# Matmuls that nobody reads, in the norms of a two-block transformer kernel

## The chip, the cores and the metric

One core of one Trainium2 chip runs the whole kernel. The metric is the device time of one execution in microseconds; the kernel before takes 1953.42 us (median of 3 runs, 1952.22 to 1953.73).

## The reference, cut to what matters

256 tokens of width 1024 go through two layers of a first block and two layers of a second block, all in float32. Ahead of nearly every large product stands an RMS norm over the 1024 channels of a token:

```python
def rms_norm(x, gain):
    xf = x.astype(jnp.float32)
    y = xf * lax.rsqrt(jnp.mean(xf * xf, axis=-1, keepdims=True) + EPS)
    return (y * gain.astype(jnp.float32)).astype(x.dtype)
...
# first block, twice: norm1, mixer (delta rule and short convolution), w_out, norm2, feed-forward
h = rms_norm(x, norm1_g);  proj = h @ w_in;  ...;  x = x + mixed @ w_out
h2 = rms_norm(x, norm2_g)
x = x + (jax.nn.silu(h2 @ ffn_w_gate) * (h2 @ ffn_w_up)) @ ffn_w_down
...
# second block, twice: three sub-layers (feed-forward, mixer, feed-forward), each of this form
def pre(x_in, i):
    return rms_norm_2(x_in, norm_pre[l, i]) * (1.0 + mod[:, i, 1]) + mod[:, i, 0]
def post_add(x_in, y, i, res_w):
    return x_in + res_w * mod[:, i, 2] * rms_norm_2(y, norm_post[l, i])
```

So there are ten norms ahead of products: four in the first block (two in each layer), six in the second (three in each layer).

## The kernel before, in words

**Order of the work.** The program is a list of steps (block, layer, kind, number), written out by hand. Each engine runs through the same list and issues its own part of each step; semaphores tie the parts together. Nothing is scheduled by a tool.

**Products.** Every weight matrix comes from memory in units of 128 x 1024. ScalarE rounds a unit to the short float32 form (`w_hi`, L983), VectorE subtracts to get the rest (`w_lo`, L1334), and TensorE multiplies high by high, high by low and low by high. In the feed-forwards (`gu` steps) one pair of matmuls does this for one block of 128 channels: 512 columns against `w_hi` (L515) and 256 columns against `w_lo` (L516); a first `gu` step has 16 such pairs. In the mixers a block takes three matmuls of 256 columns (L609 to L611 in their first step, L505 to L507 later). The sums with the tokens on the partitions (`out`, `mout`, `down`) are matmuls of 512 columns; the last of them are L545 to L547.

**A norm ahead of products** (kinds `norm` and `pre`) takes its input from such sums. VectorE adds them to `x` (L1468), or, from the second block's first feed-forward on, a `post` step does this and the norm behind it in one chain of VectorE and ScalarE. ScalarE sums the squares, VectorE scales four quarters of `x` into `xs` (L1357, a part of the tensor `mx`; in the fused chain the last quarter comes from ScalarE, L1039). TensorE turns each quarter with four transposes of 128 x 128 (L689; `q` counts the quarters). When quarter 2 is turned, ScalarE and VectorE read the turned tiles out of PSUM into `hf`, apply the gain (L1099, L1102, L1409, L1411) and split them into `h_hi` and `h_lo` (L1108, L1044, L1342). The next step's first product waits for the first `h_lo`.

**Names.** `quad` is four PSUM banks that the products of the steps use in turn; `banks[0]` and `banks[1]` count how often each half of it has been read out. `works` (also `work[0]` to `work[3]`) is the other four banks. `n["turn"]` counts the norms ahead of products (0 to 9), `FUSED` is 5: the norms of turn 5 and later follow a `post` step directly. `g_hi` is a buffer of rounded hidden values, `ident_r` the rounded identity.

Of the kernel before, what the change touches and what calls it, by code (L numbers as in the profile page):

```python
# [205 lines left out]
def build(nc, w, x_in, const_in, p1_in, p2_in, bt_in, out):  # L206
    with ExitStack() as ctx:
        def sb(name, shape, dt=F32):
            return ctx.enter_context(nc.sbuf_tensor(name, shape, dt))

        def ps(name, shape):
            return ctx.enter_context(nc.psum_tensor(name, shape, F32))
# [11 lines left out]
        g_hi = sb("g_hi", [P, 4, T], F32R)  # L224
# [17 lines left out]
        ident_r = sb("ident_r", [P, P], F32R)  # L242
# [3 lines left out]
        quad = ps("quad", [P, 4, 512])  # L246
        stream = [quad[:, 2 * i, :].rearrange("p (a t) -> p a t", a=2) for i in range(2)]
        works = ps("works", [P, 4, 512])
        work = [works[:, i, :] for i in range(4)]
# [34 lines left out]
        def turned_tile(into, kt):  # L284

            at = kt % 4 // 2 * T
            return into[2 * (kt // 4) + kt % 2][:, at:at + T]
# [113 lines left out]
        banks = [s_bank0, s_bank1]  # L401
# [8 lines left out]
        FUSED = AT[2, 0, "pre", 0]["turn"] + 1  # L410

        def scaled_before(turn):
            return 4 * turn - max(turn - FUSED, 0)

        chunks, loads = [], []
        for B, L, kind, i, n in NUMBERED:
# [5 lines left out]
            else:  # L422
                for v in range(n["split"], n["split"] + units_of(B, kind, i)):
                    if v % 2 == 0:
                        loads.append(("raw", len(chunks)))
                        chunks.append(("split", v + 2))
        chunk_of_unit = [c for c, (kind, _) in enumerate(chunks) if kind == "split" for _ in range(2)]
        chunk_of_mod = {n - 1: c for c, (kind, n) in enumerate(chunks) if kind == "mod"}
        mod_of_side = {k: m for m, k in SIDE_OF.items()}
# [65 lines left out]
        def _(pe):  # L495
            mm, tr = nc.tensor.matmul, nc.tensor.transpose
# [38 lines left out]
            def product_rows_end(unit, kts, r_hi, r_lo, sums):  # L535

                pe.wait_ge(s_lo_ready, unit + 2)
                for q in range(2 * TT):
                    for e, kt in enumerate(kts):
# [10 lines left out]
                        elif e:  # L550
                            last.then_inc(s_bank_done, 1)

            def attend(L, k, h0):

                kp, ke = k // 2, k % 2
                pe.wait_ge(s_pt_sb, AH * L + k + 1)
                if ke == 0:
                    pe.wait_ge(s_hf_done, h0 + kp)
                o = turned[64 * ke:64 * ke + 64, (kp % 2) * T:(kp % 2 + 1) * T]
                mm(o[:, 0:T], vt[:, 0, k * AD:(k + 1) * AD], pt[:, 0:T], start=True, stop=False, skip_group_check=True)  # L560
                mm(o[:, P:T], vt[:, 1, k * AD:(k + 1) * AD], pt[:, T:T + P], start=False, stop=True,
                   skip_group_check=True).then_inc(s_pe_at, 1)
# [6 lines left out]
            for B, L, kind, i, n in NUMBERED:  # L569
# [88 lines left out]
                elif kind == "grow":  # L658
# [5 lines left out]
                    for half, dst in enumerate(row_banks(B, i, n)):  # L664
                        for j in range(4):
                            kt = 4 * half + j
                            last = mm(dst[:, j * P:(j + 1) * P], gains[:, kt:kt + 1].to_broadcast([P, P]), ident,
                                      start=True, stop=True)
                        last.then_inc(s_pe_row, 1)
                elif kind == "crow":  # L670
                    pe.wait_ge(s_csil_done, 1)
                    for half, dst in enumerate((turned, work[3])):
                        for j in range(4):
                            kt = 4 * half + j
                            last = mm(dst[:, j * P:(j + 1) * P], csil[:, 1, kt:kt + 1].to_broadcast([P, P]), ident,
                                      start=True, stop=True)
                        last.then_inc(s_pe_crow, 1)
                elif kind in ("norm", "pre"):
                    into = turned_into(B, kind, i)
                    if (B, kind, i) == (2, "pre", 1):  # L680
                        pe.wait_ge(s_b0_sb, 2 * (L + 1))
                    for q in range(2 * TT):
                        if q == 3 and n["turn"] >= FUSED:
                            pe.wait_ge(s_xs3_done, n["turn"] - FUSED + 1)
                        else:
                            pe.wait_ge(s_xs_done, scaled_before(n["turn"]) + q + 1)
                        for j in range(4):
                            kt, t = 4 * (q % 2) + j, q // 2
                            last = tr(turned_tile(into, kt)[:, t * P:(t + 1) * P], xs[:, t, kt * P:(kt + 1) * P], ident)  # L689
                        if q >= 2:  # L690
                            last.then_inc(s_pe_turn, 1)
                elif kind in ("gates", "flog"):
                    pe.wait_ge(s_hhi_done, n["h"])
                    dst = work[0] if kind == "gates" else turned
                    for kt in range(DT):
                        by = p1_(L, "w_ba", kt * 8, kt * 8 + 8) if kind == "gates" else p2_(L, "w_f", kt * 8, kt * 8 + 8)
                        last = mm(dst[32 * (kt % 4):32 * (kt % 4) + 8, 0:T], by, hf[:, kt, :], start=kt < 4,
                                  stop=kt >= 4, skip_group_check=True)
                    last.then_inc(s_pe_part, 1)
                elif kind in ("gsum", "fsum"):  # L700
                    pe.wait_ge(s_part_sb, 4 * (2 * (B - 1) + L + 1))
                    dst = work[0] if kind == "gsum" else turned
# [3 lines left out]
                elif kind == "decay":  # L706
# [4 lines left out]
                    for c in range(TT):  # L711
                        for h, r, cols in heads(c):
                            last = mm(work[2 + c][:, cols], sm["g"][:, r:r + 1].to_broadcast([P, P]), triu,
                                      start=True, stop=True)
                        last.then_inc(s_pe_grow, 1)
                elif kind == "nsum":
# [5 lines left out]
                    for j in range(2):  # L722
                        pe.wait_ge(s_sq_done, n["sq"] + j + 1)
                        for e in range(2):
                            for c in range(TT):
                                k = 4 * j + 2 * e + c
                                last = mm(sums[:, k:k + 1], sq[:, j, e * T + c * P:e * T + c * P + P], ones[:, 0:1],
                                          start=True, stop=True)
# [18 lines left out]
                elif kind == "kq":  # L747
# [3 lines left out]
                    for c in range(TT):  # L751
                        for h, r, cols in heads(c):
                            last = mm(work[2 + c][:, cols], kT[:, h, c * P:(c + 1) * P], qT[:, h, c * P:(c + 1) * P],
                                      start=True, stop=True)
# [13 lines left out]
                elif kind == "lvt" and i < 5:  # L768
# [5 lines left out]
                    for r in range(8):  # L774
                        for q in quarter:
                            last = mm(work[0][q, 32 * r:32 * r + 32], lts_c[i - 1][q, r, :], xt_c[q, r, :],
                                      start=True, stop=True)
# [11 lines left out]
                elif kind == "lvt" and i == 5:  # L789
                    pe.wait_ge(s_x_upd, 8 * L + 4)  # L790
                    pe.wait_ge(s_qk_done, 2 * (L + 1))
                    for p in range(2):
                        up, low = slice(64 * p, 64 * p + 32), slice(64 * p + 32, 64 * p + 64)
                        for r in range(8):
                            last = mm(works[up, 2 * p, 32 * r:32 * r + 32], lt[low, r, up], xt_c[low, r, :],
                                      start=True, stop=True)
                        last.then_inc(s_pe_t, 1)
                elif kind == "lvx" and i == 5:
                    pe.wait_ge(s_xi_ready, 4 * (L + 1))
                    for p in range(2):  # L800
                        up, low = slice(64 * p, 64 * p + 32), slice(64 * p + 32, 64 * p + 64)
                        pe.wait_ge(s_t_sb, 8 * L + 4 + p + 1)
                        for r in range(8):
                            last = mm(works[up, 2 * p + 1, 32 * r:32 * r + 32], xi_c[up, r, :], tt5[up, r, :],
                                      start=True, stop=True)
                            if p == 0:
                                last = mm(works[low, 1, T + 32 * r:T + 32 * r + 32], tt5[up, r, :], xi_c[up, r, :],
                                          start=True, stop=True)
                        last.then_inc(s_pe_dx, 1)
                elif kind == "lvt":  # L810
# [3 lines left out]
                    for c in range(TT):  # L814
                        for h, r, cols in heads(c):
                            last = mm(works[up, 2 * c, 64 * h:64 * h + 64], lt[low, r, up], xt[low, r, low],
                                      start=True, stop=True)
                        last.then_inc(s_pe_t, 1)
                elif kind == "lvx":
                    up = slice(0, 64)  # L820
                    for c in range(TT):
                        pe.wait_ge(s_t_sb, 8 * L + 6 + c + 1)
                        for h, r, cols in heads(c):
                            last = mm(works[up, 2 * c + 1, 64 * h:64 * h + 64], xi64[up, r, :], tt6[up, r, :],
                                      start=True, stop=True)
                        last.then_inc(s_pe_dx, 1)
                elif kind == "scan":
# [23 lines left out]
                    for h in range(HEADS):  # L851
                        mm(work[h // 2][:, (h % 2) * T:(h % 2) * T + P], vn0[:, h, :], qk[:, h, :], start=h % 2 == 0,
                           stop=True, skip_group_check=True)
                    for h in range(HEADS):
                        mm(work[h // 2][:, (h % 2) * T + P:(h % 2) * T + T], s_sb[:, h, :], qdec[:, h, :], start=False,
                           stop=False, skip_group_check=True)
                    pe.wait_ge(s_vn1_done, L + 1)
                    for h in range(HEADS):
                        last = mm(work[h // 2][:, (h % 2) * T + P:(h % 2) * T + T], vn1[:, h, :], qk[:, 4 + h, :],
                                  start=False, stop=True, skip_group_check=True)  # L860
# [7 lines left out]
                elif kind == "kzero":  # L868
# [3 lines left out]
                    for st in range(ST):  # L872
                        ut, q = st // 4, st % 4
# [13 lines left out]
                elif kind == "bu":  # L887
# [4 lines left out]
                    for half in range(2):  # L892
                        if half:
                            pe.wait_ge(s_bu_half, 2 * (4 * L + i + 1))
                        for e, name in enumerate(("b_re", "b_im")):
                            for b in range(2):
                                for q in (2 * half, 2 * half + 1):
                                    rows = slice(32 * q, 32 * q + 32)
                                    a = half * T + e * BLK
# [3 lines left out]
                                              start=b == 0, stop=b == 1, skip_group_check=True)  # L903
                                    if b == 1 and e == 1:
                                        last.then_inc((s_bu_half, s_pe_bu)[half], 1)
                elif kind == "y":
# [4 lines left out]
                    for q in range(4):  # L911
                        for e in range(2):
                            mm(o[32 * q:32 * q + 32, 1, :], cp[:, 0, e, 4 * i + q, :], sst[:, e, q * BLK:(q + 1) * BLK],
                               start=e == 0, stop=e == 1, skip_group_check=True)
                    mm(o[:, 0, :], k0[:, i, :], u2[:, i, :].rearrange("p (k b) -> p b k", b=2)[:, 0, :],
                       start=True, stop=False, skip_group_check=True)
# [13 lines left out]
                elif kind == "score":  # L930
# [6 lines left out]
                    if AH * L + i > 0:  # L937
# [6 lines left out]
                       start=False, stop=False, skip_group_check=True)  # L944
# [3 lines left out]
                elif kind == "turnp":  # L948
                    pe.wait_ge(s_p_norm, 2 * (AH * L + i + 1))
                    if i == 0:  # L950
                        pe.wait_ge(s_vt_sb, 2 * (L + 1))
                    if AH * L + i > 0:
                        pe.wait_ge(s_pt_sb, AH * L + i)
                    tr(work[3][:, 0:P], pr[:, i % 2, T:T + P], ident)
                    tr(work[3][:, P:T], pr[:, i % 2, 0:P], ident)
                    tr(work[3][:, T:T + P], pr[:, i % 2, P:T], ident).then_inc(s_pe_pt, 1)
                elif kind == "attend":
                    if i == 0:
                        pe.wait_ge(s_vt_sb, 2 * (L + 1))
                    attend(L, i, AT[2, L, "hout", 0]["h"])  # L960
# [1094 lines left out]
```

## Time and profile before

| | |
|---|---|
| median of 3 runs | 1953.42 us (1952.22 to 1953.73) |
| the profiled execution | 1951.06 us, its span 1949.0 us |
| TensorE busy | 1852.7 us, 95% of the span |
| VectorE busy | 1470.2 us, 75% |
| ScalarE busy | 1069.2 us, 55% |
| mean granted TensorE clock | 0.976 of full speed |

The profile is of one execution, whose own time lies 2.36 us under the median. A group of rows below gives, for a stretch of the span, how long TensorE had an instruction running and what clock it was granted (1.00 is 2.4 GHz, 0.50 is 1.2 GHz). In a timeline the number in brackets is how long the engine sat idle before the instruction and on whom it waited.

### The profile page before, as it was taken

What the parts mean: (1) busy time and instruction counts of PE and PEld (TensorE: products, weight loads), DVE (VectorE), ACT (ScalarE), POOL (GpSimd) and SP (SyncE); (2) the same over time, 40 slices, a digit from 0 to 9 for tenths busy, and PEclk for the clock granted to TensorE, in tenths of its full rate; (3) what the DMA queues carried; (4) which work ended last, traced back from release to release, by engine and by line L of the source; (5) the groups of instructions that cost most, each with busy time, mean ns of one, the idle gap of its engine ahead of it and who ended that gap; (6) DMA issues with size and microseconds to landing.
All of it is one profiled execution on the core that took longest, in us unless ns stands there. A gap on an engine that the chain in (4) does not pass through costs nothing.

```text
span 1949.0 us, 31511 instructions
## 1 busy us (share of the span) xinstructions
PE 1852.7 (95%) x12640; PEld 1627.4 (84%) x12640; DVE 1470.2 (75%) x2334; ACT 1069.2 (55%) x1744; POOL 202.1 (10%) x174
## 2 busy tenths in 40 slices
PE   6899999998999998999799989998999899989998
PEld 5898888788888887888799978887888799978887
DVE  5756799875568987888687777998777777776555
ACT  6535555654465456656534465446566744556554
POOL 0100111111011111111000001110111100001111
PEclk9989999999999999999899989999999999999999
DMA  5333898433369864555343449984545343344552
GB/s 231 120 115 112 319 346 331 151 130 110 130 248 356 317 223 162 216 216 216 130 152 124 161 176 355 364 313 152 205 174 191 133 152 130 112 171 171 175 195 87
DMA packets 53281, 383.50 MB, mean 197 GB/s; under 512 B 5905, under 2 KB 6033, under 8 KB 6929
## 3 DMA queue, kind: packets, MB, share of 16 engines
q1 hardware_dynamic: 53136, 381.50, 52.6%
q8 instruction: 100, 1.64, 0.3%
q14 instruction: 45, 0.36, 0.1%
HBM read 380.43 MB, written 1.05 MB: 196 GB/s over the span
## 4 chain that ended last, share of the span: by engine, by line
PE 74%; DVE 13%; ACT 7%; issue 4%; DMA 2%; POOL 0%; SPq 0%; DVEq 0%; ACTq 0%
PE quad L515 20%; PE quad L516 10%; PE quad L505 6%; PE quad L506 5%; PE quad L507 5%; PE works L527 4%; PE works L529 4%; PE works L528 4%; DVE w_lo L1334 3%; ACT w_hi L983 2%; DMA raw<-w 2%; DVE mx L1480 2%; DVE mx L1519 1%; PE works L901 1%; DVE raw L1480 1%
## 5 line engine op out<-in xcount | busy, mean ns | idle before, releaser
L1334 DVE TENSOR_TENSOR w_lo<-raw,w_hi 128x1024 fp32r<-128x1024 f32 x572 | 700.3, 1232 | 215.6 <-ACT w_hi L983 213.7
L515 PE MATMUL quad<-h_two,w_hi 128*128 128x512 f32 x2112 | 759.7, 403 | 8.8 <-DVE h_two L1342 4.6
L983 ACT ACTIVATE w_hi<-raw 128x1024 fp32r<-128x1024 f32 x572 | 595.9, 1053 | 207.7 <-PE quad L516 98.2
L516 PE MATMUL quad<-h_two,w_lo 128*128 128x256 f32 x2112 | 598.0, 283 | 0.0
L515 PEld LDWEIGHTS quad<-h_two,w_hi 128*128 128x128 f32 x2112 | 402.6, 191 | 112.1 <-issue 13.5
L516 PEld LDWEIGHTS quad<-h_two,w_lo 128*128 128x128 f32 x2112 | 405.0, 192 | 1.9
L1886 POOL TENSOR_TENSOR g_lo<-hid,g_hi 128x256 fp32r<-128x256 f32 x140 | 177.2, 1267 | 1514.3 <-ACT g_hi L1048 1514.3
L505 PE MATMUL quad<-h_two,w_hi 128*128 128x256 f32 x960 | 280.1, 292 | 10.7 <-DVE w_lo L1334 10.7
L506 PE MATMUL quad<-h_two,w_hi 128*128 128x256 f32 x960 | 273.8, 285 | 0.0
L507 PE MATMUL quad<-h_two,w_lo 128*128 128x256 f32 x960 | 273.5, 285 | 0.0
L505 PEld LDWEIGHTS quad<-h_two,w_hi 128*128 128x128 f32 x960 | 186.3, 194 | 15.6 <-issue 13.9
L527 PE MATMUL works<-w_hi,g_hi 128*128 128x512 f32 x480 | 189.2, 394 | 0.2 <-DVE w_lo L1334 0.2
L529 PE MATMUL works<-w_lo,g_hi 128*128 128x512 f32 x480 | 187.7, 391 | 0.0
L528 PE MATMUL works<-w_hi,g_lo 128*128 128x512 f32 x480 | 187.2, 390 | 0.0
L506 PEld LDWEIGHTS quad<-h_two,w_hi 128*128 128x128 f32 x960 | 186.4, 194 | 0.0
L507 PEld LDWEIGHTS quad<-h_two,w_lo 128*128 128x128 f32 x960 | 186.1, 194 | 0.0
L1480 DVE CUSTOM_DVE_ANT_0 mx<-mx,crow 128x1024 f32<-128x1024 f32 x128 | 151.0, 1217 | 0.0
L1048 ACT ACTIVATE g_hi<-hid 128x256 fp32r<-128x256 f32 x140 | 57.4, 412 | 149.4 <-DVE hid L1369 145.8
L1238 ACT ACTIVATE sq<-quad 128x512 f32<-128x512 f32 x132 | 78.0, 591 | 99.7 <-PE quad L516 99.4
L1668 DVE TENSOR_TENSOR sq<-sq,quad 128x512 f32<-128x512 f32 x132 | 90.2, 683 | 54.1 <-ACT sq L1238 53.5
L529 PEld LDWEIGHTS works<-w_lo,g_hi 128*128 128x128 f32 x480 | 90.1, 188 | 20.4
L527 PEld LDWEIGHTS works<-w_hi,g_hi 128*128 128x128 f32 x480 | 90.1, 188 | 19.7 <-issue 0.5
(417 smaller groups left out, 2180.0 us busy)
## 6 DMA issues: line engine op xcount, KB each, us to landing
raw<-w SPq DMA_DIRECT2D x294, 1024.0 KB, 4.9
mx<-w SPq DMA_DIRECT2D x64, 1024.0 KB, 7.0
par<-p_in SPq DMA_DIRECT2D x2, 1110.0 KB, 7.4
x<-x_in SPq DMA_DIRECT2D x1, 1024.0 KB, 5.3
mx<-bt_in SPq DMA_DIRECT2D x2, 512.0 KB, 6.1
out<-x SPq DMA_DIRECT2D x4, 256.0 KB, 2.3
con<-const_in SPq DMA_DIRECT2D x1, 428.0 KB, 3.0
par<-p_in SPq DMA_DIRECT2D x1, 225.0 KB, 5.4
```

Of the source, the lines that this page charges most:

```text
L505: mm(o, hi, r_hi[:, kt, :], start=first, stop=False, skip_group_check=True)
L506: mm(o, hi, r_lo[:, kt, :], start=False, stop=False, skip_group_check=True)
L507: last = mm(o, lo, r_hi[:, kt, :], start=False, stop=end, skip_group_check=True)
L515: mm(o, hi, h_two[:, kt, :, :], start=kt == 0, stop=False, skip_group_check=True)
L516: return mm(o[:, 0:T], lo, h_hi[:, kt, :], start=False, stop=kt == DT - 1, skip_group_check=True)
L527: mm(sums[q][:], a_hi, hi, start=first, stop=False)
L528: mm(sums[q][:], a_lo, hi, start=False, stop=False)
L529: last = mm(sums[q][:], a_hi, lo, start=False, stop=end)
L983: f(w_hi[:, v % SLOTS, :], raw[:, chunk_of_unit[v] % RAWS, (v % 2) * UNIT:(v % 2 + 1) * UNIT], ACT.Copy).then_inc(s_hi_ready, 1)
L1334: v.tensor_tensor(w_lo[:, q % SLOTS, :], raw[:, chunk_of_unit[q] % RAWS, (q % 2) * UNIT:(q % 2 + 1) * UNIT], w_hi[:, q % SLOTS, :].bitcast ...
L1480: v.tensor_tensor_reduce(rows, rows, crow[:], 1.0, 0.0, ALU.mult, ALU.add, modacc[:, 2 * i + e:2 * i + e + 1]).then_inc(s_mod_used, 1)
L1886: v.tensor_tensor(g_lo[:, slot, :], hid[:, g % 2, :], g_hi[:, slot, :].bitcast(F32), ALU.subtract)\
```

## The change

In nine of the ten norms ahead of products (all but the first of the kernel) TensorE gets additional matmuls of 128 x 128 against 512 columns. Their operands are `ident_r` and the first two tiles of `g_hi`, whatever these hold at the time; they write a PSUM bank that the next user starts afresh, and nobody reads the result. All wait for nothing but that bank.

- The five fused norms (turns 5 to 9): 11 behind the last sum, 1 behind quarter 0's transposes, 2 behind quarter 1's, 4 behind quarter 3's: 18.
- The second block's first norm (turn 4): 20 behind the last sum, then 1, 2 and 4: 27.
- The second layer's first norm in the first block (turn 2): 6, then 1, 2 and 4: 13.
- The norms ahead of the first block's two feed-forwards (turns 1 and 3): 6 behind the last sum, into `work[3]`, and no others.

That makes 90 + 27 + 13 + 12 = 142 matmuls. Nothing is removed, and nothing changes on another engine.

```diff
+            def keep_clock(dst, count):
+                for _ in range(count):
+                    mm(dst, ident_r[:], g_hi[:, 0:2, :].rearrange("p a t -> p (a t)"), start=True, stop=True)
...
                 elif kind in ("norm", "pre"):
                     into = turned_into(B, kind, i)
                     if (B, kind, i) == (2, "pre", 1):
                         pe.wait_ge(s_b0_sb, 2 * (L + 1))
+                    keep, p = n["turn"] > 0, n["pair"] + 1
+                    beside = work[3] if (B, i) == (1, 1) else quad[:, 2 * (p % 2), :]
+                    if keep and (B, i) != (1, 1):
+                        pe.wait_ge(banks[p % 2], p // 2)
+                    if keep:
+                        keep_clock(beside, 11 if n["turn"] >= FUSED else 20 if B == 2 else 6)
                     for q in range(2 * TT):
+                        if keep and 0 < q < 3:
+                            keep_clock(beside, 0 if (B, i) == (1, 1) else q)
                         if q == 3 and n["turn"] >= FUSED:
...
+                    if keep and (B, i) != (1, 1):
+                        keep_clock(beside, 4)
```

On TensorE, a fused norm ahead of a feed-forward (`pre` 2 of the second block's first layer) reads as follows before the change: the last sums, sixteen transposes, the first products.

```order
L545 MATMUL works<-w_hi,h_two 128x512
L546 MATMUL works<-w_hi,h_two 128x512
L547 MATMUL works<-w_lo,h_two 128x512
L689 MATMUL works<-con,mx 128x128 x16
L515 MATMUL quad<-h_two,w_hi 128x512
L516 MATMUL quad<-h_two,w_lo 128x256
```

The same place after it, where the transposes' line is L701 and the added matmuls' is L555:

```order
L547 MATMUL works<-w_lo,h_two 128x512
L555 MATMUL quad<-g_hi,ident_r 128x512 x11
L701 MATMUL works<-con,mx 128x128 x4
L555 MATMUL quad<-g_hi,ident_r 128x512
L701 MATMUL works<-con,mx 128x128 x4
L555 MATMUL quad<-g_hi,ident_r 128x512 x2
L701 MATMUL works<-con,mx 128x128 x8
L555 MATMUL quad<-g_hi,ident_r 128x512 x4
L515 MATMUL quad<-h_two,w_hi 128x512
```

No instruction moved against another; eighteen stand between them. The norms ahead of the first block's feed-forwards (turns 1 and 3) read like this after the change, again on TensorE, from the last sum to the first product:

```order
L546 MATMUL quad<-w_hi,h_two 128x512
L547 MATMUL quad<-w_lo,h_two 128x512
L555 MATMUL works<-g_hi,ident_r 128x512 x6
L701 MATMUL works<-con,mx 128x128 x16
L515 MATMUL quad<-h_two,w_hi 128x512
```

Here only the six behind the last sum are new; between and behind the transposes stands what stood there before.

## Rows read from the trace of the kernel before

**Rows 1.** The page's list of engines: busy us (share of the span) xinstructions
```profile
PE 1852.7 (95%) x12640; PEld 1627.4 (84%) x12640; DVE 1470.2 (75%) x2334; ACT 1069.2 (55%) x1744; POOL 202.1 (10%) x174
```

**Rows 2.** TensorE's waits: us in total, times, longest us
```profile
PE works L689 <- DVE mx L1357: 23.5, 15, 6.0
```

**Rows 3.** Two of eight half-clock stretches around norms: us, PE busy (x), PEclk
```profile
732.44:739.27 6.83, 3.52 (x16) 0.50 0.00 0
...
1145.45:1155.69 10.24, 8.73 (x29) 0.50 0.01 2
...
sum 61.44, PE 49.90; mean PE 6.24
```

**Rows 4.** Timeline at 1141 us: start us, us, instruction [idle before]
```profile
1140.92 0.39 PE L546 MATMUL works<-w_hi,h_two 128*128 128x512 f32 x1
...
1141.15 0.39 PE L547 MATMUL works<-w_lo,h_two 128*128 128x512 f32 x1
...
1144.75 0.66 PE L689 MATMUL works<-con,mx 128*128 128x128 f32 x4 [3.21 <-DVE mx L1357]
...
1145.81 1.11 PE L689 MATMUL works<-con,mx 128*128 128x128 f32 x4 [0.40 <-DVE mx L1357]
...
1147.28 1.97 PE L689 MATMUL works<-con,mx 128*128 128x128 f32 x8 [0.35 <-DVE mx L1357]
1148.43 0.56 ACT L1102 ACTIVATE hf<-works,modv,mx 128x256 f32<-128x256 f32 x1 [0.98 <-PE works L689]
...
1150.05 0.77 PE L515 MATMUL quad<-h_two,w_hi 128*128 128x512 f32 x1 [0.80 <-DVE h_two L1342]
...
1150.82 0.63 PE L515 MATMUL quad<-h_two,w_hi 128*128 128x512 f32 x1
...
1151.46 0.63 PE L515 MATMUL quad<-h_two,w_hi 128*128 128x512 f32 x1
```

**Rows 5.** Timeline at 374 us, a norm whose clock stayed full
```profile
374.10 0.66 PE L689 MATMUL quad<-con,mx 128*128 128x128 f32 x4 [1.90 <-DVE mx L1357]
...
374.60 0.60 PE L689 MATMUL works<-con,mx 128*128 128x128 f32 x4
...
375.71 0.66 PE L689 MATMUL quad<-con,mx 128*128 128x128 f32 x4 [0.52 <-DVE mx L1357]
...
376.41 0.47 ACT L1099 ACTIVATE hf<-quad,par 128x256 f32<-128x256 f32 x1 [1.47 <-PE quad L689]
```

**Rows 6.** Timeline at 736 us, the second block's first norm
```profile
735.75 3.66 PE L689 MATMUL works<-con,mx 128*128 128x128 f32 x16 [5.97 <-DVE mx L1357]
...
738.61 0.56 ACT L1102 ACTIVATE hf<-works,modv,mx 128x256 f32<-128x256 f32 x1 [2.02 <-PE works L689]
...
740.23 0.47 PE L515 MATMUL quad<-h_two,w_hi 128*128 128x512 f32 x1 [0.81 <-DVE h_two L1342]
...
743.86 0.40 PE L515 MATMUL quad<-h_two,w_hi 128*128 128x512 f32 x1
```

**Rows 7.** Six stretches from a norm's first product to full clock
```profile
184.83:189.72 4.89, 4.89 (x15) 0.50 0.00 0
...
1754.24:1759.85 5.61, 5.61 (x17) 0.50 0.00 0
sum 28.01, PE 28.00; mean PE 4.67
```

**Rows 8.** Timeline at 930 us, last sums at half clock behind a gap
```profile
930.57 0.79 PE L545 MATMUL works<-w_hi,g_hi 128*128 128x512 f32 x1 [4.99 <-POOL g_lo L1886]
...
932.01 0.63 PE L545 MATMUL works<-w_hi,g_hi 128*128 128x512 f32 x1
932.44 0.63 PE L546 MATMUL works<-w_hi,g_lo 128*128 128x512 f32 x1
```

**Rows 9.** Timeline at 180 us, the norm of turn 1
```profile
180.88 1.09 PE L689 MATMUL works<-con,mx 128*128 128x128 f32 x8 [1.89 <-DVE mx L1357]
...
182.49 1.63 PE L689 MATMUL works<-con,mx 128*128 128x128 f32 x8 [0.52 <-DVE mx L1357]
```

## The prediction, as it was put on record

> **What bounds the kernel now.** I read the page's list of engines first. TensorE has an instruction running for 1852.7 of 1949.0 us [rows 1], far more than any other engine, so time is won only where TensorE's gaps close or where it works faster. The list of its waits names the gaps: the largest kind is the transposes (L689) waiting for VectorE's scaled quarters, 23.5 us over 15 waits for those that go to `works` alone [rows 2]. These waits cannot close by this change, since VectorE's chain is untouched.
>
> The third view is the granted clock, stretch by stretch. Around eight of the nine norms concerned it stands at 0.50, which is 1.2 GHz, for up to 10.24 us each, 61.4 us over eight stretches, of which two stand there [rows 3]. What TensorE did before shows why the norms are the place: after the last sum it stands idle (3.21 us at 1144.75), runs four transposes, waits again (0.40 us), and then the clock is down: four transposes take 1.11 us where the four before took 0.66 [rows 4]. The one norm without a fall is that at 374 us, with a shorter idle time of 1.90 us [rows 5]; but the norm at 181 us has nearly the same gaps (1.89 and 0.52 us) and falls: its second eight transposes take 1.63 us after 1.09 for the first [rows 9]. So whether the clock falls there is near an edge, and more work in the gaps should tip it. In the other direction, sixteen transposes without a gap from 735.75 on [rows 6] are all that TensorE did before its clock rose at 739.27 [rows 3].
>
> **The change part by part.** I price the whole loss around the norms first, then what of it comes back, then what the added matmuls cost. The sum is made against the profiled execution (1951.06 us, 2.36 us under the median) and the difference then applied to the median.
>
> (a) Products at half clock. In six norms the first products start while the clock is down. From the first product to the clock's return this is 28.01 us in six stretches, TensorE busy throughout [rows 7]. A pair L515/L516 takes 0.64 us there (1150.82 to 1151.46) [rows 4]. At full clock, behind the norm at 736 us where the clock was back in time, ten pairs take 3.63 us (740.23 to 743.86), 0.363 us each, with the little waiting on `h_lo` that this phase has anyway [rows 6]. So 1 - 0.363/0.64 = 43% of the 28.01 us come back: 12.1 us. For the mixer's triples I take the same ratio.
>
> (b) Transposes at half clock, on the way to the first product. From the start of quarter 2's transposes to ScalarE's first read takes 1.15 us at half clock (1147.28 to 1148.43) [rows 4] and 0.70 us at full clock (375.71 to 376.41) [rows 5]: 0.45 us a norm. This holds in the five fused norms and at turn 3: 2.7 us. At 181 us, where the fall comes during these transposes, I take 0.1 us; at 736 us, where quarters 0 and 1 are slow too, 0.5 us, as quarter 2 would start at about 737.43 instead of 737.49 and then save its 0.45 us. Together 3.3 us.
>
> (c) Cost of the added matmuls. The trace has no matmul with these operands. The nearest row is a sum with 512 columns in a row of such: start to start 0.23 us at full clock (1140.92 to 1141.15) [rows 4], its weight load beside it, and 0.43 us at half clock (932.01 to 932.44) [rows 8]. I take 0.23, since the clock is full when the last sum ends. Eleven then need 2.5 us of the 3.2 us gap, six need 1.4 us of 1.89 us [rows 9], twenty need 4.6 us of 5.97 us [rows 6]: free, as the gap covers them. At 1144.75 us four transposes issue in 0.50 us (374.10 to 374.60) [rows 5], one added matmul brings it to 1145.48, before quarter 1 at 1145.81; that is done at 1146.31, two more bring 1146.77, before quarter 2 at 1147.28. Quarter 3 then ends at 1148.28, four more end at 1149.2, and the first product, now 0.45 us earlier, comes at 1149.6. Free again. Only at 374 us do they not fit: quarters 0 and 1 come together there, so 0.50 + 0.23 + 0.50 + 0.46 = 1.69 us go by before quarter 2, which came after 1.61 us: 0.1 us lost. If a matmul took more than 0.30 us (3.3 us over eleven), the first transposes would be late; at 0.43 us each the cost is 11 x 0.13 = 1.4 us a fused norm.
>
> (d) Queues. Behind the added matmuls only TensorE's own transposes and products stand. The wait for the bank is for a read-out that lies a feed-forward's sums or more back, so it is open. The sums are signalled by the last sum itself, ahead of the added ones, so ScalarE and VectorE start as before. Beside them TensorE writes a bank that no one reads. I take nothing for contention.
>
> (e) What is late next. TensorE ran at full busy share in the stages behind the norms, so a stage that starts earlier ends earlier. The other idle spots stay: 4.99 us at 930.57, behind which the sums run at half clock, 0.43 us instead of 0.23 [rows 8]. Their falls can come a little earlier, later or not at all when all moves by some us; I put +-2 us on them.
>
> Sum: 12.1 + 3.3 - 0.1 = 15.3 us, if the clock stays up at all norms. The profiled execution would be 1935.8 us, the median 1953.4 - 15.3 = 1938.1 us.
>
> A rule bears on this. The transposes are a large part of what is left in the gaps: sixteen between the eleven and the first product. In this trace transposes alone stood ahead of the clock's rise at 739.27 [rows 3, 6]. The Trainium skill ("TensorE: Matmul & The Clock Gate", Part 4: PE-mode transpose) says that a transpose doesn't count as work on TensorE in the same way and that the full clock doesn't engage for it. By the rows the sum is the one above; by that rule it is the slower rival below. The row and the rule disagree, and I go by the row.
>
> **The rivals.**
> 1. The six matmuls of turns 1 and 3 don't hold the clock, the others do. Nothing is added between or behind their transposes, so the 0.52 us ahead of quarter 2 and the wait for the first `h_lo` stay. Against it: 374 us kept its clock with no help at all. Price: of (a), 4.89 us at turn 1 [rows 7] and about as much at turn 3 stay at half clock, 9.8 us at 43% or 4.2 us, and 0.5 us of (b): 1942.8 us.
> 2. The clock still falls in about half of the fused norms, since idle spots of 0.3 to 0.9 us remain between the added ones. Then half of the 15 us stays lost, and where it falls ahead of quarter 1 the additions cost up to the amount of rival 3: about 1947 us. If it falls as often as before, gain and cost cancel to 1953 us.
> 3. Slower than before. Transposes don't keep the clock, so the added matmuls don't either, and it is down when quarter 1 comes. At half clock four transposes issue in 0.87 us; quarter 1 from 1145.81 ends at 1146.68, two added at 0.43 us end at 1147.54, 0.26 us after quarter 2 could start; quarter 3 ends at 1149.28, four added end at 1151.0, and the product that came at 1150.05 waits 0.95 us for them. Five fused norms cost 4.8 us, that at 736 us about 1.5 us: 1953.4 + 6.3 = 1959.7 us. It decides when the clock is down at quarter 1 in four or more of them. For it speaks 1145.81, where it was down at quarter 1 [rows 4]; by the rule of the Trainium skill above this rival is what comes. Against it stands the rise at 739.27 behind transposes alone.
> 4. An added matmul takes 0.43 us or more at full clock, as its operands or a bank written again and again could make it: up to 1.4 us at each of five norms, 7 us off the gain: 1945 us. Nothing in the rows of the sums, which also write one bank three times running, speaks for it.
>
> **How the numbers follow.** All norms hold: 0.56. Rival 1: 0.16. Rival 2: 0.14, a third of it within reach of no change. Rival 3: 0.05. Rival 4: 0.05. The rest, 0.04, for what I don't see. The prediction is the first's, 1938.1 us. Below it only (e)'s 2 us and a better ratio in (a) reach: with 0.35 us a pair it is 0.6 us more, so 1935. Above it I take in rivals 1 and 4 and the mild half of rival 2: 1946. About 0.2% (3.9 us) is what a measurement of this kernel can tell from no change. Faster by more: 0.56 + 0.16 + 0.05 + two thirds of 0.14 + 0.01 = 0.87. Same: 0.07. Slower: 0.06.
>
> **What would show it.** In the changed kernel's profile the mean granted clock rises from 0.976 to about 0.99 and the stretches at 0.50 around the norms are gone. Eleven added matmuls start 0.23 us apart and end ahead of the first transposes, whose wait on L1357 shrinks to under 1 us but whose distance from the last sum (3.60 us) stays. Quarter 2 to ScalarE's first read takes 0.70 us everywhere, and pairs behind each norm are 0.36 us apart. The prediction is wrong if a 0.50 stretch still covers first products, if L555 is further apart than 0.30 us, or if a first product waits for the four behind quarter 3.

## The result, and the profile after

The changed kernel takes 1937.46 us (median of 3 runs, 1935.08 to 1938.89) against 1953.42 before: ratio 0.9916, 95% interval 0.99 to 0.9932. The forecast was 1938.1 us, within 1935 to 1946. The profiled execution of the changed kernel takes 1935.08 us with a span of 1933.0 us and a mean granted clock of 0.990 (before: 1951.06, 1949.0 and 0.976).

The page's list of engines, against [rows 1] (busy us, share of the span, instructions):

```profile
PE 1863.2 (96%) x12782; PEld 1634.4 (85%) x12782; DVE 1470.2 (76%) x2334; ACT 1069.5 (55%) x1744; POOL 202.1 (10%) x174
```

TensorE has 142 instructions and 10.5 us of busy time more, and the span is 16.0 us shorter. The 142 added ones, at 0.23 us each, are about 33 us of work. That the busy time grows by no more than 10.5 us fits the rest of the work running faster. TensorE's wait for the scaled quarters, against [rows 2] (us in total, times, longest):

```profile
PE works L701 <- DVE mx L1371: 7.1, 16, 1.3
```

23.5 us of waiting became 7.1, but the quarters come no earlier: the added matmuls now stand where the wait stood, and VectorE hands over its quarters when it did. The gain is in the clock. The stretches below begin at the last sum of each of the nine norms and are 14 us long (us, PE busy (instructions), granted clock, DMA share, GB/s):

```profile
178.43:192.43 14.00, 11.86 (x69) 1.00 0.14 47
369.27:383.27 14.00, 13.30 (x96) 1.00 0.12 36
532.53:546.53 14.00, 11.86 (x69) 1.00 0.19 56
725.57:739.57 14.00, 12.43 (x66) 1.00 0.07 27
932.94:946.94 14.00, 12.59 (x82) 1.00 0.12 49
1134.18:1148.18 14.00, 12.57 (x68) 1.00 0.10 43
1334.36:1348.36 14.00, 12.57 (x68) 1.00 0.05 20
1531.14:1545.14 14.00, 12.56 (x82) 1.00 0.07 29
1732.42:1746.42 14.00, 12.57 (x68) 1.00 0.10 43
```

All nine stand at 2.4 GHz, where [rows 3] and [rows 7] show 1.2 GHz around eight of them. The timeline at 1134 us is the norm of [rows 4] (start us, us, instruction, idle before it):

```profile
1134.18 0.39 PE L547 MATMUL works<-w_lo,h_two 128*128 128x512 f32 x1
...
1134.41 2.74 PE L555 MATMUL quad<-g_hi,ident_r 128*128 128x512 f32 x11
...
1137.78 0.66 PE L701 MATMUL works<-con,mx 128*128 128x128 f32 x4 [0.63 <-DVE mx L1371]
...
1138.84 0.66 PE L701 MATMUL works<-con,mx 128*128 128x128 f32 x4 [0.17 <-DVE mx L1371]
...
1140.31 1.09 PE L701 MATMUL works<-con,mx 128*128 128x128 f32 x8 [0.35 <-DVE mx L1371]
1141.00 0.57 ACT L1116 ACTIVATE hf<-works,modv,mx 128x256 f32<-128x256 f32 x1 [0.52 <-PE works L701]
...
1141.16 1.18 PE L555 MATMUL quad<-g_hi,ident_r 128*128 128x512 f32 x4
...
1142.62 0.47 PE L515 MATMUL quad<-h_two,w_hi 128*128 128x512 f32 x1 [0.29 <-DVE h_two L1356]
```

What to see: the first transposes start 3.60 us behind the last sum, as before, and 0.63 us of that is idle instead of 3.21. Quarter 2 starts 6.13 us behind it, as before. From there to ScalarE's first read it takes 0.69 us instead of 1.15, and the first product comes 8.44 us behind the last sum instead of 8.90. The second block's first norm, against [rows 6], and the first block's at 369 us, against [rows 5]:

```profile
725.80 4.85 PE L555 MATMUL quad<-g_hi,ident_r 128*128 128x512 f32 x20
731.93 0.66 PE L701 MATMUL works<-con,mx 128*128 128x128 f32 x4 [1.28 <-DVE mx L1371]
```

```profile
371.57 0.66 PE L701 MATMUL quad<-con,mx 128*128 128x128 f32 x4 [0.50 <-DVE mx L1371]
...
373.20 0.64 PE L701 MATMUL quad<-con,mx 128*128 128x128 f32 x4
```

At turn 4 the transposes still wait 1.28 us, and the clock holds. In the norm of turn 1, against [rows 9], the clock no longer falls between its two sets of transposes, with the same 0.52 us between them:

```profile
180.71 1.10 PE L701 MATMUL works<-con,mx 128*128 128x128 f32 x8 [0.49 <-DVE mx L1371]
182.32 1.09 PE L701 MATMUL works<-con,mx 128*128 128x128 f32 x8 [0.52 <-DVE mx L1371]
```

The changed kernel still stands at 1.2 GHz in six other stretches ahead of TensorE's last instruction. Four of them (us, PE busy, clock, DMA share, GB/s), and the gap of [rows 8], which is still there:

```profile
97.00:107.30 10.30, 8.38 (x157) 0.50 0.19 76
...
452.00:462.20 10.20, 9.12 (x131) 0.50 0.17 53
...
923.00:929.90 6.90, 4.29 (x10) 0.51 0.82 322
1281.40:1284.90 3.50, 3.44 (x11) 0.51 1.01 426
```

```profile
925.61 0.80 PE L545 MATMUL works<-w_hi,g_hi 128*128 128x512 f32 x1 [4.98 <-POOL g_lo L1900]
```

The account, stage by stage. A stage runs from the last sum ahead of one norm to that of the next; both times are starts in the timelines, such as 1141.15 before and 1134.18 after for turn 6. "Forecast" takes 43% of that norm's stretch at half clock and its share of (b). The four stretches of the kernel before that [rows 7] leaves out are those of turns 3, 5, 6 and 7 (us, PE busy, clock, DMA share, GB/s):

```profile
540.68:544.71 4.03, 4.03 (x13) 0.50 0.00 0
946.31:950.89 4.58, 4.58 (x21) 0.50 0.00 0
1150.05:1155.69 5.64, 5.64 (x17) 0.50 0.01 3
1353.82:1357.08 3.26, 3.26 (x10) 0.50 0.03 8
```

| from turn | before us | after us | change | forecast |
|---|---|---|---|---|
| start to 1 | 178.60 | 178.43 | -0.17 | 0 |
| 1 | 193.21 | 190.85 | -2.36 | -2.2 |
| 2 | 162.30 | 163.26 | +0.96 | +0.1 |
| 3 | 195.28 | 193.04 | -2.24 | -2.2 |
| 4 | 208.03 | 207.37 | -0.66 | -0.5 |
| 5 | 203.73 | 201.25 | -2.48 | -2.4 |
| 6 | 203.77 | 200.18 | -3.59 | -2.9 |
| 7 | 198.72 | 196.78 | -1.94 | -1.9 |
| 8 | 201.70 | 201.27 | -0.43 | -0.45 |
| 9 to the end | 203.66 | 200.58 | -3.08 | -2.9 |

The last row is good to 0.1 us only, as the spans are read to that.

### The profile page after: what moved, and what is told of

Same layout as the page of the kernel before. It is cut to its first block, busy times and chain, and to the rows that moved or that the text cites. A ratio compares the mean times of both kernels' runs of the same rounds, so it can differ in the third digit from the quotient of the medians.

```text
span 1933.0 us, 31795 instructions
## 1 busy us (share of the span) xinstructions
PE 1863.2 (96%) x12782; PEld 1634.4 (85%) x12782; DVE 1470.2 (76%) x2334; ACT 1069.5 (55%) x1744; POOL 202.1 (10%) x174
## 4 chain that ended last, share of the span: by engine, by line
PE 75%; DVE 13%; ACT 7%; issue 4%; DMA 2%; POOL 0%; SPq 0%; DVEq 0%; ACTq 0%
PE quad L515 20%; PE quad L516 10%; PE quad L505 6%; PE quad L506 6%; PE quad L507 6%; PE works L527 5%; PE works L529 5%; PE works L528 5%; DVE w_lo L1348 3%; ACT w_hi L997 2%; DVE mx L1494 2%; DMA raw<-w 2%; DVE mx L1533 1%; PE works L915 1%; DVE raw L1494 1%
## 5 line engine op out<-in xcount | busy, mean ns | idle before, releaser
L515 PE MATMUL quad<-h_two,w_hi 128*128 128x512 f32 x2112 | 748.2, 398 | 7.8 <-DVE w_lo L1348 3.8
```

Source lines behind the costliest of these rows:

```text
L515: mm(o, hi, h_two[:, kt, :, :], start=kt == 0, stop=False, skip_group_check=True)
```

## The experiments

All times are medians; "before" is the kernel before, run beside the other on the same chip. Its single executions range over 1948.1 to 1956.2 us, so differences of a us or two between kernels are read from stages of the traces, not from the medians. Theory: the clock is held by TensorE having work nearly all the time between the last sum and the first product, whatever the work is. Rivals: that only the gap behind the last sum counts, that only matmuls and not transposes hold it, that the added work costs something.

**Only behind the last sum.** The 11, 20 or 6 stay, the ones between and behind the transposes go.

```diff
-                            keep_clock(beside, 0 if (B, i) == (1, 1) else q)
+                            keep_clock(beside, 0)
...
-                        keep_clock(beside, 4)
+                        keep_clock(beside, 0)
```

> Of the added matmuls only those behind the last sum stay (11, 20 or 6); the 1, 2 and 4 between and behind the transposes are gone. Theory (the clock is held by work spread over the whole gap): the clock falls again in some of the five fused norms, in about half of them, each fall costing 2 to 3 us, so 1942 to 1946 us. Rival (only the long idle spot behind the last sum matters): no fall at any norm, and the time is that of the changed kernel, 1937 us.

Measured: 1938.92 us (before 1952.29), ratio 0.9936 (0.9918 to 0.9953). Of nine norms one falls, that at 1335 us (timeline):

```profile
1339.22 0.66 PE L701 MATMUL works<-con,mx 128*128 128x128 f32 x4 [0.63 <-DVE mx L1371]
1340.28 0.66 PE L701 MATMUL works<-con,mx 128*128 128x128 f32 x4 [0.40 <-DVE mx L1371]
1341.75 1.09 PE L701 MATMUL works<-con,mx 128*128 128x128 f32 x8 [0.81 <-DVE mx L1371]
1344.06 0.58 PE L515 MATMUL quad<-h_two,w_hi 128*128 128x512 f32 x1 [1.22 <-DVE h_two L1356]
```

With idle times of 0.81 and 1.22 us left, it falls at the first product, and its stage takes 198.64 us instead of 196.78. The other four fused norms, with the same idle times, hold, and so do the four other norms. Neither expectation held as it stood: about half of the five were to fall, or none. So the matmuls behind the last sum bring most of the gain, 13.4 us of some 16 against the kernel before. The others remove a risk: 1.9 us where it struck.

**Only between and behind the transposes.** The 1, 2 and 4 stay.

```diff
-                        keep_clock(beside, 11 if n["turn"] >= FUSED else 20 if B == 2 else 6)
+                        keep_clock(beside, 0)
```

> Only the 1, 2 and 4 between and behind the transposes stay, none behind the last sum. Theory: the 3.2 us of idle time behind the last sum is back, so the clock falls in all five fused norms and in that of turn 4, and where it is down the additions make quarter 2 and the first product late by up to 0.95 us: 1952 to 1957 us. Rival (the additions next to the products are what holds the clock): 1940 us or less.

Measured: 1946.19 us (before 1952.29), ratio 0.9974 (0.9965 to 0.9983): 6.1 us of some 16, which neither view had. The clock falls at seven of the nine norms, at five of them for 3.4 us only. Not all of the 6.1 us is the matmuls' work: turns 1 and 3 have none here, and still turn 3 holds its clock, with the 1.89 and 0.52 us idle that it had in the kernel before, where it fell; its stage takes 192.59 us instead of 195.28. The timeline of turn 8 shows what the fall does:

```profile
1544.54 0.63 PE L701 MATMUL quad<-con,mx 128*128 128x128 f32 x4 [3.30 <-DVE mx L1371]
...
1546.97 1.11 PE L701 MATMUL quad<-con,mx 128*128 128x128 f32 x4 [0.15 <-DVE mx L1371]
...
1548.58 1.68 PE L555 MATMUL quad<-g_hi,ident_r 128*128 128x512 f32 x4
1550.10 0.28 PE L613 MATMUL quad<-h_two,w_hi 128*128 128x256 f32 x1
```

The transposes run at 1.2 GHz (1.11 us for four), but by 1550.10 the clock is back, before the products begin. Turn 8 is a norm where it was back in time in the kernel before too. At turn 6, where it came back 5.64 us into the products (1150.05 to 1155.69), it is now back ahead of them as well, and the first takes 0.47 us instead of 0.77 [rows 4]:

```profile
1151.39 0.47 PE L515 MATMUL quad<-h_two,w_hi 128*128 128x512 f32 x1
```

The price stands in the rows of turn 8: the four behind quarter 3, at half clock, hold the first product until 9.25 us behind the last sum (1540.85), against 8.89 before. That is the wait of rival 3, in the one kernel where the clock is down at the transposes and the additions have their full width. It is 0.36 us where rival 3 took 0.95; at turn 4 the first product is 1.35 us later than before, where it took about 1.5.

**Transposes in place of the added matmuls.** The same time is covered with fp32 transposes of a constant tile: 20, 36 or 11 behind the last sum, then 2, 4 and 7.

```diff
-                    mm(dst, ident_r[:], g_hi[:, 0:2, :].rearrange("p a t -> p (a t)"), start=True, stop=True)
+                    tr(dst[:, 0:P], crow[:, 0:P], ident)
```

> Each added matmul of 512 columns is replaced by transposes of 128 x 128 in float32 that take about the same time (20, 36 or 11 behind the last sum, 2 and 4 between, 7 behind; 0.125 us each). Theory (transposes keep the clock as well as matmuls of equal duration): all norms at full clock, 1937 us within 2. Rival, the rule of the Trainium skill (TensorE: Matmul & The Clock Gate, Part 4) that transposes don't count as work: the falls of before are back and the additions come on top, 1955 to 1960 us.

Measured: 1942.34 us (before 1952.29), ratio 0.9952 (0.9934 to 0.9969). The timeline at 1139 us, where TensorE runs nothing but transposes for the 8.4 us between the last sum and the first product:

```profile
1139.84 2.35 PE L555 MATMUL quad<-con,crow 128*128 128x128 f32 x20
1143.21 0.66 PE L701 MATMUL works<-con,mx 128*128 128x128 f32 x4 [1.02 <-DVE mx L1371]
...
1148.05 0.47 PE L515 MATMUL quad<-h_two,w_hi 128*128 128x512 f32 x1 [0.46 <-DVE h_two L1356]
```

The clock stays at 1.00 at all nine norms, and the first product comes 8.44 us behind the last sum, as in the changed kernel. Transposes do hold the clock here. The time, though, missed the 1937 us within 2 that the theory gave: its median is 4.6 us over that of the changed kernel's second run (below). The trace of that run has a span 5.3 us shorter, and these 5.3 us lie in four stages: the one up to turn 1, with no added work in it, takes 180.73 us instead of 179.65 (178.43 in the changed kernel's first trace), turn 1's 191.26 instead of 190.86, turn 4's 210.08 instead of 207.81, turn 8's 202.75 instead of 201.25 with a 3.4 us stretch at 0.50 at 1570.7 us, behind the norm and its first products. Turn 4's 210 us and turn 8's 202.75 us came back in a kernel with the matmuls as they were (the mixer's part alone, below), so I don't put them on the transposes; why these stages differ stays open.

**Narrow matmuls.** The same counts, 64 columns instead of 512.

```diff
-                    mm(dst, ident_r[:], g_hi[:, 0:2, :].rearrange("p a t -> p (a t)"), start=True, stop=True)
+                    mm(dst[:, 0:64], ident_r[:], g_hi[:, 0, 0:64], start=True, stop=True)
```

> As many added matmuls at the same places, but each with 64 columns instead of 512, so that TensorE is touched as often and works little. Theory (work keeps the clock, not the number of instructions): the falls at most fused norms come back, the additions cost nothing, 1948 to 1954 us. Rival (any instruction keeps it): 1937 us.

Measured: 1950.44 us (before 1953.27), ratio 0.9986 (0.9975 to 0.9998); mean clock 0.976, as before the change. The norm at 1141 us (timeline):

```profile
1141.05 1.31 PE L555 MATMUL quad<-g_hi,ident_r 128*128 128x64 f32 x11
1144.42 1.11 PE L701 MATMUL works<-con,mx 128*128 128x128 f32 x4 [2.06 <-DVE mx L1371]
```

The clock falls at eight of the nine norms, all but turn 2, as before the change. The count is not what matters. Eleven narrow ones leave 2.06 us idle and the clock is down at quarter 0; eleven wide ones leave 0.63 us, twenty transposes 1.02 us, and it holds. Both the number of columns and the time covered are smaller here than in the other two, so which of them counts isn't shown, and the theory's "whatever the work is" is shown for full-width matmuls and transposes alone. Single executions of this kernel range from 1943.5 to 1954.8 us.

**Twice as many behind the last sum.** 22, 40 and 12.

```diff
-                        keep_clock(beside, 11 if n["turn"] >= FUSED else 20 if B == 2 else 6)
+                        keep_clock(beside, 22 if n["turn"] >= FUSED else 40 if B == 2 else 12)
```

> Twice as many behind the last sum (22, 40 and 12), the rest as in the change. Theory (0.23 us each, free as long as they fit the gap): 22 end 5.2 us behind the last sum where quarter 0 came at 3.6, and quarter 2 comes 0.75 us late in each fused norm (3.8 us), 3.0 us late at turn 4, 0.6 at turn 2, 0.1 at the others: 7.5 us slower than the change, 1945 us. Rival (the gap has room, or the additions cost more each): 1937 us, or over 1950 us.

Measured: 1946.72 us (before 1952.29), ratio 0.9973 (0.9963 to 0.9982). The norm at 1141 us (timeline):

```profile
1141.29 5.31 PE L555 MATMUL quad<-g_hi,ident_r 128*128 128x512 f32 x22
1146.44 0.60 PE L701 MATMUL works<-con,mx 128*128 128x128 f32 x4
...
1150.26 0.47 PE L515 MATMUL quad<-h_two,w_hi 128*128 128x512 f32 x1 [0.29 <-DVE h_two L1356]
```

The transposes follow without idle time, 5.38 us behind the last sum instead of 3.60, and the first product comes at 9.20 instead of 8.44 us: 0.76 us a norm. At turn 4 it is 3.15 us, at turn 2 0.65 us, and nothing at turns 1 and 3. Sum: 5 x 0.76 + 3.15 + 0.65 = 7.6 us, of the 9 us by which its median is over the changed kernel's second run. Stage by stage the fit is looser: against that run's trace turn 4's grows by 5.4 us and turn 6's by 2.0. Turn 4's has 3.0 us of waits for VectorE's `w_lo` in it instead of 0.8, and turn 6's one of 1.9 us instead of 0.9. Quarter 0 is 1.78 us late but the product only 0.76, since quarter 2 waited for its own scaling anyway. That slack is the room for error: 0.23 us each is right, and eleven fit.

**The changed kernel again**, with the narrow ones.

> The changed kernel itself, as the measure for the three beside it: 1937.5 us within 1, no fall of the clock at any of the nine norms.

Measured: 1937.74 us (before 1953.27), ratio 0.9918 (0.9904 to 0.9931). The clock holds at all nine norms, and so it does in every trace of a kernel with the full additions: seven traces, 63 norms.

**Two more gaps.** To the changed kernel are added 20 matmuls in the gap of [rows 8] and 10 in that at 1279 us, with `h_two` as operand.

```diff
+                        if (B, n["turn"], i) == (2, 7, 17):
+                            keep_clock_h(wide(n)[0], 10)
...
+                    if (B, n["turn"]) == (2, 5):
+                        pe.wait_ge(banks[n["pair"] % 2], n["pair"] // 2)
+                        keep_clock_h(quad[:, 2 * (n["pair"] % 2), :], 20)
```

> The change, and 20 such matmuls in the 5 us gap ahead of the last sums of the second block's first feed-forward and 10 in the 2.6 us gap ahead of one product step of its second (both in the first layer). Theory: the clock no longer falls there; sums that ran 4.3 us at 0.43 instead of 0.23 us each give 2.0 us back, products that ran 3.4 us at half clock 1.5 us: 3.5 us less than the change, 1934 us. Rival (the two falls are hidden behind VectorE, which is late there): same as the change.

Measured: 1936.83 us (before 1953.27), ratio 0.9915 (0.9901 to 0.9928). Three stretches (columns as above):

```profile
918.00:932.00 14.00, 13.66 (x60) 1.00 0.44 176
965.50:968.90 3.40, 3.40 (x18) 0.50 0.44 128
1278.00:1292.00 14.00, 13.80 (x70) 1.00 0.90 355
```

Both falls are gone and turn 4's stage is 1.96 us shorter than in the changed kernel's second run, as expected. But the clock now falls at 965.50, which costs turn 5's stage 1.5 us, and turn 6's gains 0.3 us instead of 1.5: a wait for VectorE's `w_lo` that ends at 1318.39 us takes 1.70 us there. Most of what is gained is given back further on, so the 1934 us of the theory missed, and the 0.9 us under the changed kernel's second run is within the spread of either.

**The mixer's gaps as well**, 12 ahead of step `lvt` 2 (a level of its triangular inverse) and 4 ahead of `nsum` 0 (sums of squares), in both first-block mixers.

```diff
+                        keep_clock_h(stat, 4)
...
+                    if i == 2:
+                        pe.wait_ge(s_kd_done, 8 * (L + 1))
+                        keep_clock_h(stat, 12)
```

> The run with two more gaps filled, and in both layers of the first block's mixer 12 more in the 3.1 us gap ahead of the second level of the triangular inverse and 4 in the 1.1 us gap ahead of the next sums of squares. Theory: the fall of 10.2 us there gets shorter in both layers; up to 3.5 us a layer is in reach, I expect 1.5 us, so 3 us less than the run with two gaps: 1931 us. Rival (what follows there is many tiny matmuls, which let the clock fall whatever stands ahead): the same as that run, 1934 us.

Measured: 1930.12 us (before 1953.27), ratio 0.9883 (0.9868 to 0.9898). The stages up to turn 1 and from turn 2 take 174.74 and 160.66 us instead of 179.41 and 163.28 in the run with the two feed-forward gaps alone. Of the two stretches the one behind 97 us is gone, the one behind 452 us has shrunk from 10.2 to 3.4 us. The expected 1931 us came, but not by the expected step: 3 us under the run with two gaps was the forecast, 6.7 us were measured.

**That kernel once more, and the mixer's part alone**, side by side.

> The kernel with both sets of matmuls (mixer and the two feed-forward gaps) once more, beside the one with the mixer's alone: 1930 us as before, with the difference between the two as the thing to read.

> This is the changed kernel with the additional matmuls in the first block's mixer (12 ahead of lvt 2, 4 ahead of nsum 0, in both layers) and without those in the two feed-forward gaps of the second block. If the feed-forward gaps are worth what they took in the run with them alone (their fall gone, but a new one behind, 0.9 us net), this kernel takes about 1931 us, 1 us more than the one with both. The rival: where the clock falls again behind a filled gap is an accident of the times, the feed-forward matmuls gain nothing or lose some, and this kernel takes 1929.5 us or less.

Measured, against 1953.1 us before: with both 1931.56 us, ratio 0.9885 (0.9868 to 0.9901); the mixer's alone 1936.53 us, 0.9915 (0.99 to 0.993). Of the mixer's part both expectations missed. Each part alone is about 1 us under the changed kernel's second run, which four or five executions of each can't tell from nothing; both together are 6.2 us under it, and 7.6 in their first run. Two stretches of the mixer-only kernel:

```profile
922.80:929.60 6.80, 5.23 (x12) 0.50 0.97 387
...
1564.50:1567.90 3.40, 3.40 (x18) 0.50 0.46 142
```

Its mixers do gain: the stages up to turn 1 and from turn 2 take 177.12 and 160.83 us. But turn 4's stage takes 210.35 us (207.11 with both parts), with 2.7 us of waits for `w_lo` in it instead of 0.9 in the changed kernel (1.8 with both parts), and turn 8's 202.75, with the fall at 1564.50. So the gains of single gaps don't add up: what is won goes partly into new falls and into waits for the rounded weights. What makes the weights late isn't shown. It is not plainly the DMA: in the 2 us around the three longest of these waits in turn 4 its share is 0.10, 0.00 and 0.76. What decides where the new falls come is not settled by these runs. The version with both parts is the fastest seen, 6 to 8 us ahead of the changed kernel.

## Why the prediction was right

- **(a) products at half clock, 12.1 us.** By stage, the gain beyond (b) is 2.25, 1.79, 2.01, 3.14, 1.49 and 2.63 us for turns 1, 3, 5, 6, 7 and 9, 13.3 us in all. All but turn 6 lie within 0.25 us of the forecast; there the 0.7 us more are in part unexplained, as the idle spot inside that stage falls for 3.4 us in both traces. Instruction by instruction, the changed kernel's turn 6 is ahead by 0.46 us at the first product and by 3.01 us where the clock of the kernel before came back; 0.35 us more come in the next 27 us, at full clock in both, for no reason that the traces show, and 0.2 us around a wait for `w_lo` late in the stage. At the other five the lead at the clock's return is within 0.1 us of what the whole stage gains: the gain is made there and kept. Less (b), the six leads at the clock's return make 12.7 us, 45% of the 28.01 us where the sum took 43%. That the price of a fall is its length times 43% also held for two falls that came new, 3.40 us at 965.50 and at 1570.7, with 1.5 us each; the one at turn 7 behind the last sum alone cost 1.9.
- **(b) the way to the first product, 3.3 us.** Measured 0.11, 0.45, 0.54, 0.47 and four times 0.45 us: 3.4.
- **(c) the added matmuls.** Start to start 0.23 us (1134.18 to 1134.41; eleven in 2.74 us), free in the gaps. Of the 0.1 us at turn 2, 0.03 showed at quarter 2 and 0.01 at the first product: 6.13 us against 6.12. Twice the number made the first products late by what this price gives.
- **(d) queues.** Nothing: in the fused norms quarter 0 comes 3.57 to 3.60 us behind the last sum, 3.60 to 3.69 before.
- **(e) other idle spots, +-2 us.** Stage 2 lost 0.96 us, as the half-clock stretch at 452 us is 10.2 us long, 6.8 before. The sums at 925.61 run at half clock for 4.3 us, 3.2 us before.
- **The rule of the Trainium skill** ("TensorE: Matmul & The Clock Gate", Part 4: PE-mode transpose), by which transposes don't count and the slower rival comes: neither the trace nor the run with transposes agrees; nine of nine norms stood at 1.00 with transposes alone.
- **The rivals.** 1: turns 1 and 3 held with six matmuls each, here and in every other kernel that had them at full width. Turn 3 also held once with none, so that these twelve are needed each time isn't shown. 2: no norm fell; with the matmuls between and behind the transposes gone, one did. 3: not here, but its mechanism stands in the run without those behind the last sum. 4: 0.23, not 0.43 us.
- **The signs it named.** All came but one: the wait on VectorE's quarters is under 1 us except at turn 4, where it is 1.28 us. Ten pairs behind turn 6 take 3.58 us, 0.36 each.
- **What it had not seen:** that the matmuls behind the last sum carry most of the gain (1938.92 us without the others).

That the two totals meet is partly luck. The span fell by 16.0 us where the sum said 15.3, since turn 6's 0.7 us more and the better ratio in (a) were nearly offset by the 0.96 us that stage 2 lost. The forecast also took the falls of one trace of the kernel before as given, while executions of the same kernel differ by some us; the 0.6 us between 1938.1 and 1937.46 says nothing.

## What to carry to other kernels

Where the engine that bounds a kernel idles for some us and the profile shows its granted clock down behind the gap, price the gap by the length of the half-clock stretch with real work in it (here 43% of it), not by the idle time. Work that nobody reads, issued behind the last real instruction and ended before the next input is there, cost nothing in these norms and brought that back. Transposes held the clock as matmuls did, too many made the first product late, and the narrow ones left the falls at eight of nine norms. Read the whole trace after each gap filled, since new falls and the next engine's lateness took part of the gain, and both sets of gaps together were worth more than the single sets added up.

## What the runs showed of the hardware that was not expected

The clock also falls with no idle time at all. The changed kernel's first mixer (columns as above):

```profile
112.00:138.00 26.00, 26.00 (x457) 1.00 0.36 123
138.00:141.40 3.40, 3.40 (x21) 0.50 0.00 0
```

TensorE is busy for all of the 26 us ahead of it. Among the instructions ahead of the fall are small ones, as the timeline shows:

```profile
135.51 1.84 PE L741 MATMUL quad<-con,sq 128*128 128x1 f32 x16
...
137.28 1.21 PE L830 MATMUL works<-mx 64*64 64x64 f32 x14
```

The stretches at 138 and 493 us, with the same work ahead, fall in the kernel before too; the first does in all twelve traces, whatever was added elsewhere. That the small matmuls are the cause is argued from where they stand; no run took them away. A second thing: turn 2 of the kernel before held its clock with 1.90 and 0.52 us idle [rows 5] where turn 1 fell with 1.89 and 0.52 us [rows 9], in the run with the matmuls behind the last sum alone one of five fused norms fell, with the idle times of the others, and turn 3, with the same idle times and nothing added, fell in the kernel before and held in the run with the matmuls between and behind the transposes. Near the edge, the same idle times go either way.
